# Decay differences of a chunked scan: running sums broadcast by transfers and subtracted on GpSimd, in place of mask products on TensorE

## The reference, cut to what matters

```python
acum = jnp.cumsum(dt * a_neg.reshape(G, R), axis=2)
causal = jnp.tril(jnp.ones((chunk, chunk), dtype=bool))
seg = acum[:, :, :, None] - acum[:, :, None, :]
decay = jnp.exp(jnp.where(causal[:, :, None, None], seg, -jnp.inf))
cb = jnp.einsum('bclgn,bcsgn->bclsg', Cm, Bm)
wts = cb[..., None] * decay * dt[:, :, None]
y_diag = jnp.einsum('bclsgr,bcsgrp->bclgrp', wts, x)
```

## Time and profile before

| | us |
|---|---|
| runs of the kernel, median of 3 | 1540.96 |
| lowest and highest run | 1536.28, 1543.88 |
| profiled execution, first to last instruction (span) | 1537.1 |
| PE busy in it | 1423.8 |
| DVE, ACT, POOL busy in it | 553.7, 388.6, 440.8 |

### The profile page before, as it was taken

How to read it: one execution, slowest core, us unless ns; L and a number is a source line. 1 busy time by engine, 2 the same in 40 slices (tenths; PEclk the granted TensorE clock), 3 DMA queues, 4 the chain that set the end, 5 groups by cost and what they waited for, 6 DMA issues and landing times.

```text
span 1537.1 us, 24023 instructions
## 1 busy us (share of the span) xinstructions
PE 1423.8 (93%) x9182; PEld 1217.2 (79%) x9182; DVE 553.7 (36%) x782; ACT 388.6 (25%) x581; POOL 440.8 (29%) x382
## 2 busy tenths in 40 slices
PE   6999999999998999999899699999789999999990
PEld 5999999998678759768776699964678878878870
DVE  3344420045447546545754511102531111111115
ACT  4211134443234234323423411101211101111112
POOL 5244433344235324423532433310010010010002
PEclk7899999999999999999999899999879999999995
DMA  5133322352044016105302232458139999998925
GB/s 134 42 82 82 82 69 82 82 138 55 1 115 123 15 41 156 55 0 138 100 14 59 71 82 82 124 162 332 61 135 340 341 340 335 341 344 331 341 102 198
DMA packets 179226, 220.04 MB, mean 143 GB/s; under 512 B 9193, under 2 KB 150633, under 8 KB 170943
## 3 DMA queue, kind: packets, MB, share of 16 engines
q1 hardware_dynamic: 166666, 183.20, 37.4%
q0 software_dynamic: 5040, 17.83, 3.7%
q10 hardware_dynamic: 7486, 18.56, 3.2%
HBM read 192.27 MB, written 27.30 MB: 143 GB/s over the span
## 4 chain that ended last, share of the span: by engine, by line
PE 79%; DVE 11%; issue 4%; DMA 3%; SPq 2%; ACT 2%; DVEq 1%; POOL 0%; ACTq 0%; POOLq 0%
PE acc L515 34%; PE pT L791 8%; PE pS L791 7%; PE acc L721 4%; PE acc L798 4%; DVE area L969 4%; PE pY L652 2%; PE pS L609 2%; PE pY L798 2%; PE acc L783 2%; PE pO L641 2%; PE acc L667 2%; PE pO L798 2%; SPq L421 1%; DMA ring<-in_w_in 1%
## 5 line engine op out<-in xcount | busy, mean ns | idle before, releaser
L515 PE MATMUL acc<-h_parts,ring_parts 128*128 128x328 f32 (+1 forms) x3840 | 549.4, 304 | 9.1 <-POOL ring_parts L1517 4.4
L515 PEld LDWEIGHTS acc<-h_parts,ring_parts 128*128 128x128 f32 x3840 | 532.8, 190 | 25.2 <-issue 22.2
L1517 POOL TENSOR_TENSOR ring_parts<-ring,ring_parts 128x1024 fp32r<-128x1024 f32 x104 | 259.6, 2496 | 431.1 <-ACT ring_parts L1283 431.1
L1283 ACT ACTIVATE ring_parts<-ring 128x1024 fp32r<-128x1024 f32 x104 | 110.1, 1058 | 370.2 <-PE acc L515 342.4
L791 PEld LDWEIGHTS pT<-big,area 128*128 128x128 f32 x1024 | 118.5, 195 | 8.7 <-issue 7.6
L791 PE MATMUL pT<-big,area 128*128 128x96 f32 x1024 | 118.4, 277 | 0.9 <-ACT big L1453 0.9
L515 PE MATMUL acc<-u_parts,ring_parts 128*128 128x264 f32 (+1 forms) x640 | 110.5, 301 | 0.0
L515 PE MATMUL acc<-area_parts,ring_parts 128*128 128x264 f32 (+1 forms) x512 | 93.2, 304 | 11.8 <-DVE u_parts L1047 11.8
L515 PEld LDWEIGHTS acc<-u_parts,ring_parts 128*128 128x128 f32 x640 | 97.5, 190 | 0.0
L969 DVE SCALAR_TENSOR_TENSOR area<-area,xvec 128x616 f32<-128x616 f32 x72 | 90.1, 1252 | 10.5 <-DVE area L967 0.6
L1665 POOL COPY idx<-ids 96x1 int32 x32 | 5.7, 178 | 304.6 <-PE acc L783 304.6
(11 more groups left out here) (296 smaller groups left out, 1627.5 us busy)
## 6 DMA issues: line engine op xcount, KB each, us to landing
ring<-in_w_in SPq DMA_DIRECT2D x80, 512.0 KB, 4.0
area<-in_w_gate SPq DMA_DIRECT2D x24, 1024.0 KB, 5.5
area<-in_w_up SPq DMA_DIRECT2D x24, 1024.0 KB, 8.7
area<-in_w_down SPq DMA_DIRECT2D x24, 1024.0 KB, 10.7
y_first<-big ACTq DMA_DIRECT2D x32, 384.0 KB, 7.9
area<-in_state_ssm SPq DMA_DIRECT2D x16, 512.0 KB, 7.0
out<-area SPq DMA_DIRECT2D x16, 512.0 KB, 6.5
ring<-in_w_ssd_out SPq DMA_DIRECT2D x16, 512.0 KB, 3.8
```

The source lines that it names most:

```text
L515: m = nc.tensor.matmul(acc[a][:, h, 0:n], w[s][:, k, :], x[:, k, h * HALF:h * HALF + n], start=first and k == 0 and w is w_hi and x is hi, ...
L1283: a_.activation(w_hi[b % 2], w_raw[b % 2], ACT.Copy).then_inc(hi_done, 1)
L1517: gp.tensor_tensor(w_lo[b % 2], w_raw[b % 2], w_hi[b % 2].bitcast(F32), ALU.subtract).then_inc(lo_done, 1)
```

## The change

The running sums are now computed once, ahead of the scan: PE multiplies the log-decays with the mask for all 32 heads (five more matmuls), ACT copies them out (as `acum`, tokens on partitions, which takes the place of `da`, and as `acum_t`, heads on partitions), and ACT's queue writes `acum_t` to a scratch tensor `acum_rows` in DRAM. In the scan, SP reads for each tile the running sums of eight heads back, the same row into every partition (`load_row`, 512 KB for a tile of 128 rows), into one of two slots of `wts`. POOL subtracts in place (one instruction of 128 x 1024 a tile), ACT takes Relu and then the exponential with scale -1, in place, DVE multiplies all eight heads at once. The mask products L1590 and L609 are gone, and so is the wait of ACT on PE for them.

```diff
             def load_group(g, last):
+                def load_row(i):
+                    r = ROWS[i]
+                    if i == 1:
+                        hold(sp, s_rm, g + 1)
+                    else:
+                        hold(sp, p_y, g * 5 + (1 if i == 0 else i))
+                    src = acum_rows[:, bass.ds(g * (HPG * r) + HEADS * P * i, HPG * r)]
+                    sp.dma_start(wts[0:r, i % 2, 0:HPG * r], src.broadcast_to([r, HPG * r])).then_inc(row_of[i % 2], 16)
                 for k in range(GK):
                     load_block(g_block(g, 2 + k), k, w_in_cols(g * GW + (COL_X + k * P), P))
+                load_row(0)
+                load_row(1)
                 hold(sp, hs_out, g * 64 + 1)
...
                 for k in range(GK):
                     load_block(g_block(g, 6 + k), k, w_in_cols(g * GW + (COL_Z + k * P), P))
+                    if k >= 2:
+                        load_row(k)
                 if last:
                     load_gates(0)
                 else:
                     load_cb(g + 1)
+                load_row(4)
...
+            sp.wait_ge(acum_out, 16 * TILES)
@@ PE, ahead of the scan
+                rows = pT[0:HEADS, i * P:i * P + r] if i < 4 else pS[0:HEADS, HEADS:HEADS + r]
+                nc.tensor.matmul(rows, d_i, le[0:r, 0:r], start=True, stop=True)
@@ PE, in a tile
-                    for q in range(2):
-                        if q == 1 and i < 3:
-                            pe_block(pe, g_block(g, 7 + i), 7 + i, hT_hi, hT_lo, part=0)
-                        pe.wait_ge(s_r, g * 10 + (2 * i + q + 1))
-                        pe.wait_ge(s_exp, g * 10 + (2 * i + q + 1))
-                        if q == 0:
-                            pe.wait_ge(s_st, g * 6 + (i + 1))
-                        nc.tensor.matmul(pS[0:r, 0:4 * r], gt[0:r, 0:r], rbuf[0:r, q, 0:4 * r],
-                                         start=True, stop=True).then_inc(p_seg, 1)
+                    if i < 3:
+                        pe_block(pe, g_block(g, 7 + i), 7 + i, hT_hi, hT_lo, part=0)
+                    pe.wait_ge(s_st, g * 6 + (i + 1))
...
@@ ACT, ahead of the scan
+            a_.activation(acum[:, :, :], pY[:, 0:160].rearrange(f3, h=HEADS), ACT.Copy)
+            a_.activation(acum_t[0:HEADS, 0:4 * P], pT[0:HEADS, :], ACT.Copy)
+            a_.activation(acum_t[0:HEADS, 4 * P:T], pS[0:HEADS, HEADS:HEADS + R4], ACT.Copy).then_inc(s_dta, 1)
+            act.wait_ge(s_dta, 8)
+            for i in range(TILES):
+                dst = acum_rows[0, HEADS * P * i:HEADS * (P * i + ROWS[i])].rearrange("(h l) -> h l", h=HEADS)
+                act.dma_start(dst, acum_t[0:HEADS, tok(i)]).then_inc(acum_out, 16)
@@ ACT, in a tile
-                    act.wait_ge(p_y, g * 5 + (i + 1))
-                    for q in range(2):
-                        act.wait_ge(p_seg, g * 10 + (2 * i + q + 3))
-                        a_.activation(wts[0:r, q, 0:4 * r], pS[0:r, 0:4 * r], ACT.Exp).then_inc(s_exp, 1)
+                    act.wait_ge(s_r, g * 5 + (i + 1))
+                    w = wts[0:r, i % 2, 0:HPG * r]
+                    a_.activation(w, w, ACT.Relu).then_inc(s_neg, 1)
+                    act.wait_ge(s_neg, g * 5 + (i + 1))
+                    a_.activation(w, w, ACT.Exp, scale=-1.0).then_inc(s_exp, 1)
@@ POOL
-                decays(0, 0)
-                decays(0, 1)
+                    per_group, first = row_loads(i)
+                    hold(pool, row_of[i % 2], g * per_group + first)
+                    w = wts[0:r, i % 2, 0:HPG * r].rearrange("p (h c) -> p h c", h=HPG)
+                    gp.tensor_tensor(w, acum[0:r, i, bass.ds(g * HPG, HPG)].unsqueeze(2).broadcast_to([r, HPG, r]), w,
+                                     ALU.subtract).then_inc(s_r, 1)
+                decays(0)
                 split_lo(g_block(g, 6), 6)
...
+                decays(1)
+                split_lo(g_block(g, 7), 7)
...
+                split_lo(g_block(g, 8), 8)
+                decays(2)
+                split_lo(g_block(g, 9), 9)
+                decays(3)
+                decays(4)
```

More of the change, by code:

```diff
@@ L87, in build @@
         sdec = sb("sdec", [R4, HEADS])
+        acum = da
         dg = sb("dg", [P, GK, 2])
@@ L165, in build @@
         sg, _ = carve(0, [3, T])
+        acum_t, _ = carve(4 * T, [T])
         WE = 3 * 2048
@@ L251, in build @@
         s_hist, s_tail, s_cvd, s_silu = (sem(n) for n in ("s_hist", "s_tail", "s_cvd", "s_silu"))
-        p_xt, p_cb, p_seg, p_yo, p_y, p_sn, p_yt = (sem(n) for n in ("p_xt", "p_cb", "p_seg", "p_yo", "p_y", "p_sn", "p_yt"))
+        p_xt, p_cb, p_yo, p_y, p_sn, p_yt = (sem(n) for n in ("p_xt", "p_cb", "p_yo", "p_y", "p_sn", "p_yt"))
+        acum_out, s_neg = sem("acum_out"), sem("s_neg")
+        row_of = [sem("row_of0"), sem("row_of1")]
         s_u, s_y1, s_y2, s_xd, s_cb, s_bt, s_r, s_exp, s_w, s_st = (
@@ L279, in build @@
         f_back, f_add = sem("f_back"), sem("f_add")
-        f_w, f_id, f_cast, f_x, f_tr, f_xe, f_gu, f_silu, f_act, f_dn, f_ye, f_out, f_skip = (
-            sem(n) for n in ("f_w", "f_id", "f_cast", "f_x", "f_tr", "f_xe", "f_gu", "f_silu", "f_act", "f_dn", "f_ye",
-                             "f_out", "f_skip"))
+        f_w, f_id, f_cast, f_x, f_dn, f_out, f_skip = (
+            sem(n) for n in ("f_w", "f_id", "f_cast", "f_x", "f_dn", "f_out", "f_skip"))
         g_in = [sem(f"g_in{i}") for i in range(TILES)]
@@ L310, in hold, with row_loads @@
             eng.sem_inc(held[id(eng)], 1)
+        def row_loads(i):
+            return 48 if i % 2 == 0 else 32, 16 * (i // 2 + 1)
         def conv_tile(turn, c):
@@ L648, in _ @@
                     pe.wait_ge(s_xd, g * 5 + (i + 1))
-                    pe.wait_ge(s_w, g * 10 + (2 * i + 2))
+                    pe.wait_ge(s_w, g * 5 + (i + 1))
                     pe.wait_ge(s_u, g * 5 + (i + 1))
                     for h in range(HPG):
-                        m = nc.tensor.matmul(pY[0:r, h * HD:(h + 1) * HD], wts[0:r, h // 4, (h % 4) * r:(h % 4 + 1) * r],
+                        m = nc.tensor.matmul(pY[0:r, h * HD:(h + 1) * HD], wts[0:r, i % 2, h * r:(h + 1) * r],
                                              xdt[0:r, i % 2, h * HD:(h + 1) * HD], start=True, stop=True)
@@ L996, in _ @@
                         v.tensor_copy(df[:, :, :].rearrange("p k s -> p (k s)"), pT[:, 0:32]).then_inc(s_df, 1)
-                    for q in range(2):
[L998 to L1001, removed]
+                    dve.wait_ge(s_exp, g * 5 + (i + 1))
+                    w = wts[0:r, i % 2, 0:HPG * r].rearrange("p (h c) -> p h c", h=HPG)
+                    v.tensor_tensor(w, w, cbm[0:r, 0:r].unsqueeze(1).broadcast_to([r, HPG, r]), ALU.mult).then_inc(s_w, 1)
                     if i < 4:
@@ L1583, in _, with decays @@
                     tail(c)
-                def decays(i, q):
+                def decays(i):
                     r = ROWS[i]
-                    le = m_le if i < 4 else m_le4
-                    hold(pool, p_seg, g * 10 + (2 * i + q + 1))
-                    gp.tensor_tensor(rbuf[0:r, q, 0:4 * r].rearrange("p (h c) -> p h c", h=4),
-                                     le[0:r, 0:r].unsqueeze(1).broadcast_to([r, 4, r]),
-                                     da[0:r, i, bass.ds(g * HPG + 4 * q, 4)].unsqueeze(2).broadcast_to([r, 4, r]),
-                                     ALU.mult).then_inc(s_r, 1)
@@ L1595, in _ @@
-                decays(0, 0)
-                decays(0, 1)
-                split_lo(g_block(g, 6), 6)
-                for i in range(1, TILES):
-                    for q in range(2):
-                        decays(i, q)
-                    if i < 4:
-                        split_lo(g_block(g, 6 + i), 6 + i)
-                    if i == 1:
-                        hold(pool, s_silu, g * 6 + 8)
-                        gp.tensor_copy(cmask[:, 0:LASTP], cT[:, 4 * P:TP])
-                        diag = cmask[:, R4 + LASTP:R4 + LASTP + NSEQ * (R4 + SLEN)].rearrange("p (s c) -> p s c", c=R4 + SLEN)
-                        gp.tensor_copy(diag[:, :, 0:SLEN], cT[:, TP:T].rearrange("p (s c) -> p s c", c=SLEN)).then_inc(s_cm, 1)
+                    per_group, first = row_loads(i)
@@ L1610, in _ @@
+                gp.tensor_copy(cmask[:, 0:LASTP], cT[:, 4 * P:TP])
+                diag = cmask[:, R4 + LASTP:R4 + LASTP + NSEQ * (R4 + SLEN)].rearrange("p (s c) -> p s c", c=R4 + SLEN)
+                gp.tensor_copy(diag[:, :, 0:SLEN], cT[:, TP:T].rearrange("p (s c) -> p s c", c=SLEN)).then_inc(s_cm, 1)
+                split_lo(g_block(g, 8), 8)
[3 more added lines that the diff above has]
+                decays(4)
                 hold(pool, s_bt, g * 5 + 5)
-                hold(pool, p_seg, g * 10 + 12)
+                hold(pool, p_y, g * 5 + 5)
```

36 lines of the change are left out of this document (17 added, 19 removed).

## The result

The changed kernel takes 1587.74 us (median of 4 runs, 1581.41 to 1591.83) against 1541.0 for the kernel before. The ratio is 1.032, 95% interval 1.030 to 1.035: slower by some 47 us, on the side that was forecast (1558), but 2.7 times as far and outside the range 1540 to 1573.

The account below looks back on a forecast made before the run. PE was taken to bound most of the chain, some 31 us of it L609. Terms -7.7, +6.0, +14.8, -0.8 and +1.1 gave +13.4; with +4 for the clock, +17.4, so 1558 us, range 1540 to 1573.

Parts of the forecast that it names:

- Removed from PE, tile 0: Tile 0 loses two L609 products: -1.7 us in group 0, -2.0 in the others, -7.7 in all.
- Moved, SP's list: Tile 1: block 9 queues behind a row load that waits for tile 0; 14.6 against 13.1 us, +6.0 in all.
- 0.26 and 0.71: Tile 1, in us: SP's wake-up, and the cost of the row load in front of block 9.
- the landing of 5.2: Tile 1: a 512 KB transfer issued closely behind another lands in 5.2 us, so block 9 arrives at T0+6.2.
- the pause of 3.3: Tile 1: PE, ready for L615 at T0+5.2, waits 3.3 us.
- Moved, POOL's list: Tile 2: POOL splits late block 10 before subtracting; 16.8 against 13.1 us, +14.8 in all.
- the subtraction: POOL's subtraction in tile 2: 1.9 to 2.4 us, taken as 2.1.
- Tile 3: Its row is there but POOL is late; 8.4 against 8.61 us, -0.2 a group, -0.8 in all.
- Start of tile 4: DVE's chain from L1015 to the mask product, claimed unchanged at 4.5 us.
- The clock: PE's clock falls in four of twelve places, 2.6 us each, less than half of them on the path: +4.
- the one of 3.04: A PE pause of 3.04 us in the old profile, from which PE came back at full clock.
- the clock falls twice in a group: Rival: eight falls of 2.6 us, +34 in all, 1575 us; 15% together with slower landing.

Follow-up runs that it names:

- e1: The changed kernel with SP's list reordered: blocks 9 and 10 issued ahead of row load 2, block 11 ahead of row load 3; 1561.96 us, ratio 1.016.
- b1: The kernel before with two waits alone in SP's list: block 9 waits for tile 0's end, block 10 for tile 1's; 1548.95 us, ratio 1.007.
- a1: The changed kernel with only POOL's order put back: subtractions of tiles 2 and 3 ahead of splitting blocks 10 and 11; 1584.29 us, ratio 1.030.
- e6: As e1, with spare PE products: two and two in tile 3, three ahead of tile 4's first; 1531.81 us, ratio 0.996.
- e3: As e2, with spare PE products: two and one in tile 3, three ahead of tile 4's first; 1521.79 us, ratio 0.990.
- e2: As e1, but POOL subtracts for tiles 2 and 3 ahead of splitting blocks 10 and 11; 1533.45 us, ratio 0.997.
- e4: As e3, with 24 spare products of 128x328 ahead of each group's tile 0; 1512.81 us, ratio 0.984.

## Why the prediction was wrong, by its own steps

*Removed from PE, tile 0.* -2.0 in groups 1 to 3: measured -1.9, -2.2, -1.8. Right. In group 0 -0.2 and not -1.7, for its tile 0 now began at half clock too (L619 takes 1.11, behind a pause of 3.70).

*Moved, SP's list.* The mechanism was right in each link: 0.26 and 0.71 were 0.24 and 0.65, the landing of 5.2 was 5.40, the pause of 3.3 was 3.46. In groups 1 and 3, where the clock stayed full in tile 1, the tile took 14.7 and 14.6, against 14.6 forecast; in groups 0 and 2 half clock added 1.9 (16.7 and 16.5). Shown by e1, where tiles 1 and 2 take 11.4, and by b1, where the wait alone costs.

*Moved, POOL's list.* 16.8 forecast for tile 2, 17.4 measured; the subtraction took 1.9, the lower bound. Right in size. But a1, without this move, still took 16.7 in the mean: the late block, at half clock behind its pause, would have held the tile nearly as long. PE's own work was not "done by 13.0", as the prediction had it: in group 0 its second half of the block ended 14.8 after the tile's start, only 0.4 ahead of DVE's weights.

*Tile 3.* 8.4 forecast, 10.4 measured. L668 took 3.65 in place of 1.75, which is nearly the whole difference.

*Start of tile 4.* It was costed at nothing ("unchanged, 4.5"), and what follows it "keeps its order". The order did stay, but two things changed that no order shows: L673 ran at half clock (+0.9), and POOL's mask product moved in time, beside DVE's copy (+0.7 in most groups). +1.9 a group. And its long part, with not one of PE's instructions changed, took 16.2 in place of 13.9.

*The clock: the step that failed.* It was priced at +4, by a fall in four of twelve places (tiles 1 to 3 of four groups), each costing 2.6, "less than half of them on the path". The clock was at half in ten of these twelve, and in tile 4 of every group too, where the prediction looked for none. The price of one fall was about right: 1.9 in tile 1 (16.7 and 16.5 against 14.7 and 14.6), 1.9 and 0.9 over tile 3 and the start of tile 4, 2.4 in the long part. Adding up those on the path gives an estimate of some 25 us in place of 4.

The count failed by two errors. First, it looked at single pauses and compared them with the one of 3.04 that had stayed full. But in tile 3 of group 0 the clock fell in the second of two pauses of 2.00 and 1.44, with work of 1.10 between them. Second, it looked for falls only where the change made PE wait in tiles 1 to 3. In tile 4 the removal of the mask products left PE one pause of 3.03 where it had had 0.61 and 0.42; in groups 0, 2 and 3 the clock, back since tile 3, fell a second time there, and in group 1 it had not come back at all.

Clearing tiles 3 and 4 of half clock gives 26 us between e1 and e6, and filling the changed kernel's pauses gave back 15.5 with an imperfect fit. The rival "the clock falls twice in a group" (1575) named the mechanism and took 21 us for it. It was too low by 13: some 4 for the clock, and the rest for smaller terms, since tile 0 gained 6.1 and not 7.7, tile 2 lost 17.1 and not 14.8, and the start of tile 4 lost some 3 to DVE's copy beside POOL.

What stays open: in e6 and e3 half of the 10 us between them is not placed (tile 0 was 12.5 and 11.7, with no difference in the code ahead of it). How far a1's clock would have recovered with filled pauses wasn't tried. And what decides whether the clock falls behind a given set of pauses is not shown: in e2 it fell in two groups and held in two.

## What to carry to other kernels

A transfer that must wait for a compute engine holds back everything behind it on its queue: put it behind the loads that are already free to go (here worth 26 us, by reordering SP's list alone), and look at a queue's order with the times of the waits in hand. Taking work from TensorE is worth its time only where TensorE is the one that others wait for; where it already pauses, less work there can make the rest slower. So when a change thins out TensorE's work, read the granted clock of the stretch behind it too, and test with spare products in the pauses: if the kernel gets faster by doing more, and the granted clock of these stretches is back at 1.00, the clock was the cost.

## What the runs showed of the hardware that was not expected

- A stretch of PE busy 7.0 of 8.6 us kept its clock at 1.00; one of 7.0 busy in 10.4, with no pause above 2.0, had 0.77. Tile 4's long part, 15 us of unbroken work behind a pause of 3.03, came out at 0.80.
- The same code with the same pauses (2.00 and 0.68) kept its clock in groups 2 and 3 of e2 and lost it in groups 0 and 1.
- Spare products made a kernel faster: 30 us between e1 and e6, 11.7 between e2 and e3, 9 between e3 and e4, 5.9 in the kernel before.
- A row read from one 4 KB line of DRAM into 128 partitions landed in 4.5 us in the median, no sooner than a weight block of the same size (4.0).
- A DVE copy with a single input slowed from 0.41 to between 1.08 and 1.73 beside a POOL product of 1.91.
